# One activation table for logarithm and exponential, named ahead of the logarithms of an encoder layer

## The reference

```python
proj = rms_norm(h, mix_norm) @ w_in
att  = mla_group(...)      # 8 heads, latent q and kv each with an rms_norm, softmax in chunks of 64
rw   = rwkv7_group(...)    # 8 heads of 64: a recurrence over time
h = h + concat([att, rw]) @ w_out
h = h + mem_cross_attention(rms_norm(h, ca_norm), rms_norm(mem, mem_norm), wq, wkv, wo)
h = h + squared_relu_mlp(rms_norm(h, mlp_norm), w_up, w_down)
return rms_norm(h, final_norm)
```

```python
def rms_norm(x, g): return x * rsqrt(mean(x * x) + eps) * g
# in rwkv7_group, per head:
w_log = -softplus(-(w0 + tanh(w_l) @ w2)) - 0.5 ; decay = exp(-exp(w_log))
a = sigmoid(a0 + a_l @ a2) ; g = sigmoid(g_l) @ g2
kk = kk / max(sqrt(sum(kk * kk)), 1e-12)
y = (y - mean(y)) * rsqrt(var(y) + GN_EPS) * ln_w + ln_b
```

## Time and profile before

| | |
|---|---|
| median of three runs | 1792.85 us (1786.72, 1792.85, 1793.59) |
| profiled execution, its own time | 1794.48 us |
| its span | 1792.7 us |
| ScalarE busy | 794.7 us (44%) |
| VectorE busy | 989.2 us (55%) |
| GpSimd busy | 692.6 us (39%) |
| mean granted clock of TensorE | 0.973 |

### The profile page before, as it was taken

The page is one execution under the profiler, slowest core; times in us unless marked ns, Lnnn a source line. Parts: engine busy times, 40 slices in busy tenths (PEclk is TensorE's granted clock), DMA queues, the critical chain, the costliest instruction groups (busy, mean ns, idle before and its releaser), DMA issues.

```text
span 1792.7 us, 30026 instructions
## 1 busy us (share of the span) xinstructions
PE 1720.8 (96%) x11960; PEld 1309.6 (73%) x11960; DVE 989.2 (55%) x1551; ACT 794.7 (44%) x1519; POOL 692.6 (39%) x502
## 2 busy tenths in 40 slices
PE   7999999998988888999999999999999999999997
PEld 4766666665565666778888768878888888888886
DVE  6542332325474765544340552488857765884788
ACT  5313323235343443531121322467566666756663
POOL 2211202010130211313523103398686775968772
PEclk9999999987988998999999999999999999999999
DMA  5101000000212114142201002111202022030202
GB/s 207 48 24 33 24 33 13 21 5 18 54 20 43 35 42 119 37 177 82 70 24 47 24 1 70 71 49 47 84 30 76 24 71 71 24 95 24 71 1 95
DMA packets 81681, 94.36 MB, mean 53 GB/s; under 512 B 53648, under 2 KB 56208, under 8 KB 81552
## 3 DMA queue, kind: packets, MB, share of 16 engines
q1 hardware_dynamic: 81552, 92.56, 16.6%
HBM read 82.57 MB, written 9.98 MB: 52 GB/s over the span
## 4 chain that ended last, share of the span: by engine, by line
PE 84%; DVE 7%; DMA 3%; ACT 2%; issue 2%; POOL 1%; SPq 1%; DVEq 0%; ACTq 0%; POOLq 0%
PE PS L1672 33%; PE PS L933 17%; PE PS L993 8%; PE PS L1094 3%; PE PS L1112 2%; PE PS L1133 2%; PE PS L1619 2%; PE PS L1597 2%; PE PS L1167 1%; PE PS L1457 1%; PE PS L1472 1%; PE PS L1170 1%; DMA xt_dram<-sc_s 1%; PE PS L1301 1%; DMA H<-xt_dram 1%
## 5 line engine op out<-in xcount | busy, mean ns | idle before, releaser
L1672 PE MATMUL PS<-memr,wsp 128*128 128x512 f32 x1332 | 319.9, 391 | 2.4 <-POOL wsp L894 2.4
L933 PE MATMUL PS<-xn,wsp 128*128 128x512 f32 x1344 | 309.8, 392 | 5.9 <-DVE xn L2232 5.9
L933 PEld LDWEIGHTS PS<-xn,wsp 128*128 128x128 f32 x1344 | 253.6, 189 | 61.9 <-DVE xn L2232 4.7
L1672 PEld LDWEIGHTS PS<-memr,wsp 128*128 128x128 f32 x1332 | 249.7, 188 | 57.7 <-POOL wsp L894 3.3
L775 POOL CAST wsp<-wraw 128x1024 fp32r<-128x1024 f32 x40 | 43.2, 1080 | 466.5 <-PE PS L933 305.1
L1672 PE MATMUL PS<-memr,wraw_r 128*128 128x512 f32 x684 | 165.6, 391 | 0.7 <-POOL wraw_r L894 0.7
L894 POOL TENSOR_TENSOR wsp<-sa,wsp 128x512 fp32r<-128x512 f32 x86 | 115.1, 1341 | 89.9 <-ACT wsp L2123 89.8
L993 PE MATMUL PS<-xn,wsp 128*128 128x512 f32 x576 | 146.7, 401 | 3.2 <-DVE proj L2281 3.1
L1672 PEld LDWEIGHTS PS<-memr,wraw_r 128*128 128x128 f32 x684 | 128.3, 188 | 29.1 <-POOL wraw_r L894 1.1
L993 PEld LDWEIGHTS PS<-xn,wsp 128*128 128x128 f32 x576 | 104.4, 188 | 40.1 <-issue 20.2
L1796 ACT ACTIVATE H<-PS,mst 128x128 f32<-128x128 f32 (+3 forms) x64 | 47.4, 741 | 185.2 <-DVE mst L2362 180.1
(11 more groups left out here) (349 smaller groups left out, 3161.6 us busy)
## 6 DMA issues: line engine op xcount, KB each, us to landing
wraw<-in_weights_dram SPq DMA_DIRECT2D x40, 512.0 KB, 3.5
sa<-in_weights_dram SPq DMA_DIRECT2D x32, 512.0 KB, 4.2
H<-in_x_dram SPq DMA_DIRECT2D x16, 512.0 KB, 6.3
sbx<-in_weights_dram SPq DMA_DIRECT2D x32, 256.0 KB, 2.9
sa<-in_weights_dram SPq DMA_DIRECT2D x32, 256.0 KB, 2.7
H<-in_weights_dram SPq DMA_DIRECT2D x8, 512.0 KB, 6.3
out_dram<-sbx SPq DMA_DIRECT2D x16, 256.0 KB, 2.1
a_dram<-H SPq DMA_DIRECT2D x16, 128.0 KB, 2.5
```

What stands on the lines that cost most here:

```text
L933: last = nc.tensor.matmul(PS[:, 2 * k + half, :], wsp[:, k, kt, a, :], src[:, at, b, HALF * half:HALF * half + HALF], start=(i == 0 and (a ...
L1672: last = nc.tensor.matmul(PS[:, g % PS_BANKS, :], w[:, a, win(k)], x[:, b, :], start=(k == 0 and (a, b) == (0, 0)), stop=(k == ROWS - 1 an ...
```

## The change

`preload_act_table_set` puts a load of the table with the given name into ScalarE's list. It is put at five places: ahead of the squares of the first norm, ahead of the latent norms, and ahead of step 6 of every preparation and of every pair end. The one-column Ln of L1734 is taken out.

```diff
+            nc.scalar.preload_act_table_set("natural_log_exp_and_others")
             for kt in range(KT):
                 act.wait_ge(x_loaded[kt], 16)
 ...
             act.wait_ge(eps_made, 1)
-            nc.scalar.activation(small[:, 41:42], small[:, 40:41], ACT.Ln)
 ...
+            nc.scalar.preload_act_table_set("natural_log_exp_and_others")
             latent_factor(0, "kv", KVR, mP[0])
 ...
+                if s == 6:
+                    nc.scalar.preload_act_table_set("natural_log_exp_and_others")
                 if s in (6, 7):
                     r_at(P_PE, f"ks{s - 6}_{n}")
 ...
+                if s == 6:
+                    nc.scalar.preload_act_table_set("natural_log_exp_and_others")
                 if s in (6, 7):
                     r_at(O_PE, f"vs{s - 6}_{m}")
```

## The result

| | before | after |
|---|---|---|
| median | 1792.45 us (20 runs, 1785.32 to 1795.31) | 1799.29 us (20 runs, 1787.44 to 1803.34) |
| profiled execution: time, span | 1794.48, 1792.7 us | 1801.29, 1799.5 us |
| ScalarE busy | 794.7 us | 780.5 us |
| mean granted clock | 0.973 | 0.971 |

The ratio is 1.0035, with an interval of 1.0022 to 1.0048: slower by 0.35%, some 6 us. Forecast was 1791.8 us within 1784.5 to 1796.5, so both the sign and the range were missed. A second measurement, under the experiments, gave 1.0043 (1.0026 to 1.0060). ScalarE did lose its 14.2 us of work (14.3 forecast), and the kernel got slower all the same.

A forecast was written before the change was run, and what follows sets the result against it. TensorE, busy 96% of the span, was taken as the bound. Gains of 0.32 us (first preparation) and 0.74 us (memory norm), others 0, made 1.06 us off the 1792.85 median: 1791.8 us, range 1784.5 to 1796.5.

The forecast's parts named there:

- the new Tanh load: At L1836, at worst three new loads ahead of Tanh, each fitting into ScalarE's wait for TensorE, 5.30 us at shortest.
- First norm: L2239 comes 1.29 us earlier, but GpSimd's L777 holds VectorE's L2232, so 0 us gained; bounds 0 and 1.29.
- Latent norms: Two Exp come 1.29 us earlier, but projections feed TensorE without a gap: 0 us; lost cover at most 1.28.
- First preparation: Beside the last two attention heads, Exps no longer wait for loads: 0.32 us gained; bounds 0 and 2.57.
- Memory norm: Load between Ln and Exp goes; TensorE's wait before L1288 shrinks from 1.16 to 0.42 us: 0.74 gained, bounds 0 and 1.28.
- Sum of gains: Over the whole kernel, 0.32 us in the first preparation plus 0.74 in the memory norm, other terms 0: 1.06 us.
- The first norm did not pass its gain on: Rival at the first norm: GpSimd starts second or its hold is not the cause; gain 2.35 us, 1790.5; chance 0.24.
- saved ScalarE time did not count as such: Rival for the whole kernel: every load saved is time saved, 14.3 us, giving 1778.5; chance 0.04.
- Doubled loads: Rival: old loads remain and 10 named ones come on top, 39 in all; some 4 us slower, 1797; chance 0.05.
- The clock rival: A shift moves where TensorE's clock falls or rises, seen at 395 to 420 us: 5 us either way; chance 0.12.
- its slower half: Clock falls elsewhere with 10 us more dense work at half clock: 5 us slower, 1796.8; half of the 0.12 chance.

The follow-up runs named there:

- the late loads mended: Changed kernel plus a load of the exponential's table named ahead of the first Tanh's waits in preparations 2 to 4: 1789.57 us (0.9984), repeated 1788.84 us (0.9978).
- the waits swapped: Changed kernel with the two waits of a preparation's first Tanh exchanged, TensorE's product first, VectorE's old result second: 1793.64 us, ratio 1.0005 to the kernel before.
- the late load alone: Kernel before plus a load of the already loaded table behind the waits of the first Tanh in preparations 2 to 4: 1801.42 us, ratio 1.0048.
- the preparations undone: Changed kernel without the named table in the preparations, kept in first norm, latent norms and pair ends: 1792.2 us, ratio 1.0003 to the kernel before.
- the run with the hold lifted: Kernel before with GpSimd's second low part of the weights waiting until VectorE wrote all eight low parts of the first norm: ratio 1.0005.

## Why the prediction was wrong

**The step that failed** is the new Tanh load: "at L1836 ScalarE waited 5.30 us for TensorE in the shortest of three cases, and the load fits there". It rested on the point of reading that "a load starts as soon as the instruction ahead of it on ScalarE is through, not when the activation behind it may start". All loads of the trace before did so, but at none of them did an open wait stand on its own ahead of the load. The load of L1837 came behind the wait for L1167, so none of the waiting time could hide it. The term taken as 0 measured 2 x 1.28 us of wait and some 4 to 8 us of clock, 6 to 10.9 us together. The Trainium skill, "ScalarE: Activation LUTs", section "Step-by-step: what each stage is for", says that the load is placed right before the activation. The trace after the change agrees (load at 564.39, Tanh at 565.69, nothing between). That would have spoken against my reading: right before the activation is behind a wait that stands on its own.

I also looked at the wrong neighbour. I asked how long ScalarE waits ahead of this Tanh. What decides is how long TensorE can go on without it, and in the third and fourth preparation TensorE has only the next L1167, which wants this very Tanh.

**What held**, step by step:

- First norm, 0: L2239 came 1.48 us earlier, where 1.29 were forecast, the low part started earlier and stretched, and it ended where it had.

```profile
20.17 2.47 DVE L2244 SCALAR_TENSOR_TENSOR tmp<-H,vec,PS 128x1024 f32<-128x1024 f32 x2 [3.52 <-ACT PS L1741]
22.56 3.39 DVE L2237 TENSOR_TENSOR xn<-tmp,xn 128x1024 fp32r<-128x1024 f32 x1
25.98 1.28 DVE L2244 SCALAR_TENSOR_TENSOR tmp<-H,vec,PS 128x1024 f32<-128x1024 f32 x1
```

 It took 3.39 us where 3.1 were forecast, and the next slice began at 25.98, behind which the second low part starts at 27.18 in both traces. GpSimd's instruction began at 22.52, ahead of it by 0.04 us and not 0.25, so the 0 was a near thing.
- Latent norms, 0: TensorE's products there are the same 143 of L993 in 34.2 us, with 0.2 us idle ahead, in both traces. The single Tanh load (L1768) ran at 85.18 with no wait behind it.
- First preparation, 0.32: its maximum is 1.50 us earlier (423.17 for 424.67 in the earlier trace rows; the clock had risen sooner, 0.84 and 0.70 from 410 to 420 us for 0.50), its Exp 1.81 earlier. The difference, 0.31, is the step's.

```profile
423.17 1.09 DVE L2367 TENSOR_REDUCE mst<-PS 128x1 f32<-128x896 f32 x1 [0.77 <-PE PS L1097]
424.30 1.01 ACT L1797 ACTIVATE H<-PS,mst 128x896 f32<-128x896 f32 x1 [1.79 <-DVE mst L2367]
...
428.83 1.11 ACT L1797 ACTIVATE H<-PS,mst 128x1024 f32<-128x1024 f32 x1
```

- Memory norm, 0.74: the wait ahead of L1288 went from 1.16 to 0.45 us, 0.71.

```profile
736.50 0.45 PE L1288 MATMUL PS<-sc_s,sc_w 64*64 64x64 f32 x8 [0.45 <-ACT sc_s L1903]
```

- Sum of gains, 1.06: with the late loads mended the kernel ran 1.65 and 3.8 us under the one before (0.9984 and 0.9978). With the waits swapped it ran level with it (1.0005, 0.9992 to 1.0017). The forecast gain, a ratio of 0.9994, lies within these intervals or at their edge, so the times neither confirm nor refute it; the rows above carry it.

**The rivals.** The first norm did not pass its gain on, and saved ScalarE time did not count as such. Doubled loads did not come: 18, not 39. The clock rival had the sign and about the size of the clock part (5 us of 4 to 8), but I gave it a place (395 to 420 us) and a cause (a shift) that were not it; from 395 to 505 us the mean clock was 0.79 before and 0.82 after. 0.06 for its slower half was far too little, because I had not joined it to the step that could leave TensorE idle. The two prices belong together, a wait of TensorE and the clock behind it.

## What to carry to other kernels

Here a table load that nobody named stood directly in front of its activation, behind the wait named last and ahead of the one named first, which the activation carries; that was tested at one activation with two waits. In a trace, look at the idle time ahead of each load, and name the table ahead of the waits where the engine has slack. When a change brings a new load or wait, ask not how long its own engine was idle there but who wants the result, and what that engine has to do meanwhile. Where TensorE is the bound, price an idle gap of a microsecond with the clock that it may lose behind it: here two steps longer by 1.28 us each cost 6 to 11 us together, 3 to 5 each.

## What the hardware showed beyond that

- A gap of 1.4 us in TensorE's work was followed by some 10 us at the half clock in four of seven cases: in the changed kernel at both places, in its repeated run at one of two (564.60 us yes, 642.27 us no), in the kernel with the late load alone at one of two (565.13 no, 635.13 yes), and not at the one place left with the preparations undone (632.12). Three filling products in the gap, and the clock stayed at 1.00 behind it in the profiled execution. What decides between the cases is open; where the clock had just been at the half level it sometimes fell again and sometimes did not.
- A lead of 0.04 us was enough for GpSimd to hold VectorE up: L777 began at 22.52, VectorE's low part at 22.56, and the low part took 3.39 us for 1.22 of work and ended 1.08 us after L777. The Trainium skill, "SBUF — State Buffer", section "SBUF: two separate sides", states the rule of the pair of ports that the two engines share: whichever starts first has it for its whole instruction. These rows agree, and so does the run with the hold lifted (1.23 us).
- A load of a table that is already there takes its full time (1.28 us at 488.99 in the kernel before with one repeated load).
